# A decoder block on one core: leaving out the dummy matmuls between the output projection and the first expert's products

## The reference, cut to what matters

```
x = x + merged @ w_out
h = rmsnorm(x, norm_ffn)
logits = h @ w_router + b_router             # 256 x 32
top_val, top_idx = top_k(logits, 4)
gates = softmax(top_val)
for every expert e and its tokens:           # 32 experts
    gate, lin = split(h[toks] @ w_gu[e] + b_gu[e])
    act = (lin + 1) * min(gate, 7) * sigmoid(1.702 * gate)   # lin clipped to +-7
    y = act @ w_down[e] + b_down[e]
out = rmsnorm(x + sum over the 4 experts of gates * y)
```

## Time and profile before

| what | value |
|---|---|
| time, median of 3 runs | 1159.8 us (1159.04 to 1160.73) |
| profiled execution, own time | 1161.07 us |
| profiled execution, span from first to last instruction | 1159.3 us |
| granted TensorE clock, mean over the span | 0.998 |
| PE busy | 1128.6 us (97%) |
| DVE, ACT, POOL busy | 320.7, 202.8, 20.6 us |
| DMA | 442.99 MB, 382 GB/s over the span |
| chain that ended last | PE 69%, DMA 23%, DVE 4% of the span |

### The profile page before, as it was taken

The page is one execution under the profiler, slowest core; times in us unless marked ns, Lnnn a source line. Parts: engine busy times, 40 slices in busy tenths (PEclk is TensorE's granted clock), DMA queues, the critical chain, the costliest instruction groups (busy, mean ns, idle before and its releaser), DMA issues.

```text
span 1159.3 us, 14630 instructions
## 1 busy us (share of the span) xinstructions
PE 1128.6 (97%) x5910; PEld 495.7 (43%) x5910; DVE 320.7 (28%) x559; ACT 202.8 (17%) x290; POOL 20.6 (2%) x25
## 2 busy tenths in 40 slices
PE   8999999999999999999999999999999999999996
PEld 6998999553333333333233333333333322222232
DVE  5689755141112211111111111111111111111112
ACT  3464433110111011101010111101010101010002
POOL 0020002000000000000000000000000000000000
PEclk9999999999999999999999999999999999999999
DMA  9956536979999999999999999999999999999995
GB/s 306 244 205 253 171 121 252 366 307 411 430 427 428 430 429 427 430 428 430 428 428 430 428 427 430 428 429 429 428 430 428 427 430 428 429 429 428 429 425 224
DMA packets 48048, 442.99 MB, mean 382 GB/s; under 512 B 4728, under 2 KB 8344, under 8 KB 23192
## 3 DMA queue, kind: packets, MB, share of 16 engines
q1 hardware_dynamic: 46248, 439.13, 92.0%
q10 hardware_dynamic: 1776, 3.52, 0.9%
HBM read 441.19 MB, written 1.44 MB: 382 GB/s over the span
## 4 chain that ended last, share of the span: by engine, by line
PE 69%; DMA 23%; DVE 4%; SPq 1%; ACT 1%; issue 1%; DVEq 0%; POOLq 0%; POOL 0%; ACTq 0%
PE psum L895 25%; DMA qk_silu<-in_w_gu 17%; PE psum L927 16%; DMA ring<-in_w_down 4%; PE psum L860 4%; PE psum L875 4%; DMA ring<-in_w_in 2%; PE psum L834 2%; DVE slot_r L1247 2%; PE psum L906 2%; PE psum L554 2%; PE psum L561 2%; PE psum L556 2%; PE psum L914 1%; PE psum L869 1%; PE psum L675 1%
## 5 line engine op out<-in xcount | busy, mean ns | idle before, releaser
L895 PE MATMUL psum<-ring,hT_region 128*64 128x512 f32 x1280 | 289.6, 594 | 11.3 <-DMA ring<-in_w_gu 10.7
L927 PE MATMUL psum<-ring,hT_region 128*64 128x512 f32 x768 | 175.3, 598 | 3.0 <-DMA ring<-in_w_down 3.0
L895 PEld LDWEIGHTS psum<-ring,hT_region 128*64 128x64 f32 x1280 | 89.7, 137 | 199.8 <-issue 177.2
L1565 DVE TENSOR_SCALAR hT_region<-psum 128x512 f32<-128x512 f32 x32 | 22.1, 692 | 398.3 <-PE psum L895 398.3
L1179 ACT ACTIVATE va_region<-hT_region 128x512 f32<-128x512 f32 x32 | 20.1, 629 | 418.2 <-DVE hT_region L1565 418.2
L927 PEld LDWEIGHTS psum<-ring,hT_region 128*64 128x64 f32 x768 | 51.0, 136 | 93.7 <-issue 90.3
L1503 DVE TENSOR_TENSOR hT_region<-psum,tiny 128x512 f32<-128x512 f32 x32 | 22.1, 692 | 204.4 <-PE psum L869 204.4
L860 PE MATMUL psum<-work,idx_region 128*64 128x512 f32 x256 | 68.8, 617 | 0.0
L1247 DVE TENSOR_TENSOR slot_r<-ring,slot_r 128x2048 fp32r<-128x2048 f32 (+1 forms) x21 | 62.2, 2971 | 23.2 <-ACT slot_r L1036 17.9
L875 PE MATMUL psum<-x_sb,idx_region 64*128 64x512 f32 x264 | 65.6, 615 | 0.7 <-ACT x_sb L1188 0.7
L895 PE MATMUL psum<-qk_silu,hT_region 128*64 128x512 f32 x256 | 58.5, 598 | 1.0 <-DMA qk_silu<-in_w_gu 0.9
(11 more groups left out here) (263 smaller groups left out, 1077.9 us busy)
## 6 DMA issues: line engine op xcount, KB each, us to landing
ring<-in_w_gu SPq DMA_DIRECT2D x79, 2048.0 KB, 25.6
ring<-in_w_down SPq DMA_DIRECT2D x47, 2048.0 KB, 21.0
bias_vb<-in_w_gu SPq DMA_DIRECT2D x16, 2048.0 KB, 26.6
qk_silu<-in_w_gu SPq DMA_DIRECT2D x16, 2048.0 KB, 27.3
hg<-in_w_down SPq DMA_DIRECT2D x16, 2048.0 KB, 31.2
sig_ab<-in_w_gu SPq DMA_DIRECT2D x16, 2048.0 KB, 28.8
ring<-in_w_in SPq DMA_DIRECT2D x12, 1024.0 KB, 5.2
ring<-in_w_in SPq DMA_DIRECT2D x5, 2048.0 KB, 15.6
```

The source lines that it names most:

```text
L895: last = mm(psum[half * 64:half * 64 + 64, b, :], xgT_sb[:, a:a + SLOTS], slot_gu(p, c, b, half)[:, jj], start=(j == 0), stop=(j == NJ - 1 ...
L927: last = mm(psum[half * 64:half * 64 + 64, 2, :], actT_sb[:, a:a + SLOTS], slot4(DOWN_HOME[p][m // 4])[:, m % 4, half * 512:(half + 1) * 5 ...
```

## The change

The five calls of `keep_warm` after `h2_transposes(1)` are left out, 15 dummy matmuls in all. The call in the transposes of the input stays. Nothing else changes.

```
             router(0)
             h2_transposes(1)
-            keep_warm(2, 1)
             router(1)
-            keep_warm(6, 3)
             pe.wait_ge(sel_ready, NT)
...
             mm(psum[:, 1, 2 * NE:3 * NE], ones, sel[:, 1, :], start=False, stop=True,
                skip_group_check=True).then_inc(pos_mm, 1)
-            keep_warm(3, 3)
...
             gather(0)
             pe.wait_ge(pick_ready, 1)
             gather(1)
-            keep_warm(2, 0)
             pe.wait_ge(last_trip_ready, 1)
             last_trip = pe.value_load(table[0:1, 2 * TAB:2 * TAB + 1], ...)
             pe.wait_ge(xg_rows_ready, 1)
             gather_T()
-            keep_warm(2, 0)
             pe.wait_ge(moe_bias_in, 128)
```

## The result

The changed kernel takes 1163.01 us, median of 20 runs (1159.99 to 1165.48), against 1159.88 us for the kernel before, median of 20 (1158.37 to 1161.98): a ratio of 1.0026, 95% interval 1.0019 to 1.0032. It is 3.1 us slower. Its runs also spread over 5.5 us, where those of before spread over 3.6.

The account below looks back on a forecast made before the run. DMA of expert weights was taken as the bound, its stream counted from the first expert's products. A clock fall of +1.3 us less 0.12 gained gave +1.2, 1161.0 us against the median; range 1158.9 to 1163.2.

Parts of the forecast that it names:

- The chain and the place: Router to first gate chunk: DVE's L1503, followed back to `router(1)`, sets its start at 248.90; first reload follows at 252.76.
- The gaps before the four groups: Sign: PE's gaps before L850, L860, L869 and L895 grow to about 1.9, 0.7, 0.7 and 0.9 us.
- Time in PE's order: Dummies ahead of chain members on PE: 0.09 us gained at `router(1)`, 0.03 at L895, 0.12 in sum.
- The clock falls: Around the gather, TensorE's clock drops from 2.4 to 1.2 GHz without the dummies; held likelier, 2 in 3.
- The price: Matmuls at half clock: 1.0 us for half of the gather's price, 0.3 for small ones around it, +1.3 us.
- the worst sum that I allowed: Gather and first gate chunk both slow: 1.2 us plus at most 3.5 for the chunk, 1164.5 us at worst.
- the likeliest case of the forecast: Clock falls once, around the gather: +1.2 us, 1161.0, own range 1160.0 to 1162.2, chance 0.50.
- the third case: Rival, chance 0.18: late or double fall also slows the first gate chunk, 248.90 to 252.4: +2.9 us, 1162.7.
- The delay reaches the end one for one: Expert stream of about 853 us: a shift of the first products' start arrives at the end nearly one for one.
- The cover: Past the first reload: a slow second or third chunk costs nothing up to about 1 us.
- The chances: Whole kernel, measured against about 0.2%: faster 0.03, same 0.76, slower 0.21.

Follow-up runs that it names:

- experiment 1: Kernel before with only the six dummies at L846 out: 1161.8 us against 1159.98, ratio 1.0016; with these six alone kept: 1160.35 us, ratio 1.0001.
- the third profile: The changed kernel itself, profiled once more with nothing altered: a single run of 1163.16 us.
- the second profile of the changed kernel: The changed kernel itself, profiled again with nothing altered: 1162.88 us against 1159.98 for the kernel before, ratio 1.0027.
- experiment 6: Kernel before with 14 dummies in place of 2 behind the transposes of the gathered rows: 1161.03 us against 1159.63, ratio 1.0012.
- the eight runs at 0.993: Eight of the changed kernel's 20 result runs, those with a mean granted clock of 0.993: median 1163.97 us, 4.1 above before.
- experiment 2: Kernel before without the six dummies at L846, the other nine kept, profiled a second time: a single run of 1163.78 us.

## Why the prediction was right, and where it was not

**The chain and the place.** Right: who sets the start of the gate products, the full buffers, and the hole in the stream of reloads that ends with it. After the change the DMA share is 0.02 from 249.50 to 254.70, and from 300 to 1100 us every stretch of 50 us moves 428 or 429 GB/s. The gaps before the four groups grew to 1.86, 0.73, 0.70 and 0.94 us, as listed.

**Time in PE's order: 0.12 us of gain, bounds 0 to 0.3.** It was 0. `router(1)` follows DVE's copy by 239.24 - (238.40 + 0.69) = 0.15 us, not by the 0.06 that I had read at another handoff; before the change it was the same 0.15, so there was nothing to gain. L889 follows L1497 by the same 0.14 as before, so no dummy stood in the way there. The kernel with the six alone kept has 13.49 us from `router(1)` to the first reload, like before.

**The clock falls: 2 in 3.** It fell in all four profiles of the changed kernel, and in none of the six profiles of kernels that keep the six dummies at L846 (before, and five of the experiments). The row that I had weighed it by, 2.2 us without a matmul at the end, was a poor guide to how little is enough: the longest idle gaps here were 1.86 us (none and nine kept), 1.34 (two kept) and 0.90 (four kept). The Trainium skill (TensorE: Matmul & The Clock Gate, HAM oscillation) ties the fall to an unbroken idle gap longer than any of these; these runs disagree with it, and the measurement decides. What exactly makes the clock fall was not found; it fell in the wait ahead of the position matmuls (the changed kernel's first profile), in the wait behind them (four kept), or while PE was at work (experiment 1).

**The price: +1.3 us, half of the gather and 0.3 for the rest.** This is the term that failed. It was mis-sized: the clock did not come back in the middle of the gather but stayed low through all of it, and in three of the four profiles through the position matmuls too: +1.75 and +0.63, so 2.4 in place of 1.3 in two profiles, and 5.3 in the two in which the first gate chunk was caught as well. The upper bounds that I had listed for the single terms (1.94 for the gather, 0.9 for the position matmuls, 0.6 for the transposes, 3.5 for the chunk) hold; halving them had no row behind it, and the worst sum that I allowed, 1.2 + 3.5, was short of the 5.3 at the first reload. So the likeliest case of the forecast (1161.0, at most 1162.2) was too low. The time came out near the middle value of the third case (1162.7), but that is partly luck: this case's mechanism, the first gate chunk at 1.2 GHz while the queues stand empty, is seen in two of four profiles and, going by their mean clock, in 8 of 20 runs, and the median of 1163.01 is that of a mixture of two cases that I had not foreseen. It lies 0.2 us inside the upper end of the range. The Trainium skill (the same page, Terms) prices a low stretch at half of its length. For the third profile, low from about 241.5 to 255, that makes an estimate of 6.8 us. The first reload came 5.33 late: for part of the stretch PE stood waiting for other engines (0.73, 0.70 and 0.94 us in the rows of that profile), and these waits are as long as they are at full clock.

**The delay reaches the end one for one, counted from the first reload.** In size about right, in place not. The fifth reload, which SP issues when PE is done with the first half of the down products, is the last at which the queues run thin: from 274 to 280 us of the profile before they move 352 to 393 GB/s, from 280 to 318 us 401 to 451. From its landing on, the stream is rigid: to PE's last wait it is 822.2 to 822.8 us in all fourteen profiles, where from the first reload it is anything from 851.7 to 855.0. In the profile before it lands 9.7 us after issue, at 283.5, and PE's last wait ends 822.2 us later; in the changed kernel it lands 11.7 us after issue, at 287.8, and the last wait ends 822.3 us later. How long the fifth takes to land (8.6 to 11.7 us over the fourteen profiles) changes between executions of one kernel. It makes up the 2.0 us by which PE's last wait moved more than the first reload did in the profile after, and it is no effect of the change: the second profile of the changed kernel has 10.0 us. What makes it long or short was not found.

**The cover.** I counted 1.04 us at L906 and 1.5 us between reloads as cover for the later chunks only. It covers the first chunk as well, as far as the fifth reload goes: 2.12 us of delay there became 1.02 (experiment 6), and 5.33 became 4.22, about the 4.1 us that the eight runs at 0.993 cost. That kept the bad case from costing its full price.

**The chances.** I had put 0.76 on no change that a measurement can tell. The change came out slower by 0.26%, just beyond the 0.2%; for slower I had 0.21.

## What to carry to other kernels

Dummy matmuls that hid behind another engine's work were free here (ratio 1.0001 with nine fewer), and one group of them was worth more than all the others: look for the longest wait of PE just ahead of matmuls that a chain hangs on, and fill that. Filling it with four dummies in place of six was worth nothing that shows. Price a fall of the clock by the whole of what stands behind it up to the point where the end is decided, not by half of it, and find that point first: here it was the landing of the fifth reload, the last place where the queue of transfers ran thin, and not the first reload.

## What the runs showed of the hardware that was not expected

The clock can go while PE does short work with short gaps: with four dummies kept, the gaps were 0.90 and 0.73 us. It can also go after the gap is over, while PE is at work (experiment 1). The same kernel does not always fare the same: the changed one was at 0.50 from 242.50 to 249.00 in the first profile, and from 242.00 to 254.50 in the third. And it can stay low through dense work: in the third profile the gather, the transposes and most of the first gate chunk ran at 0.50. Dummies that are hidden at full clock come out of hiding at half clock (1.63 us for three, experiment 2), so a filler in front of a critical matmul can make a fall dearer: 2.86 us to the first reload with these three, 2.37 without.
